# Row rings of seven and eight in place of six and six, a 4 KB descriptor scratch, and routing phases ten slots earlier

## The chip, the cores and the metric

The kernel runs on one core of one Trainium2 chip. The metric is device time in microseconds (us) from start to end of one execution; the lower, the better. Besides the tensor engine (PE), the core has a vector engine (DVE), a scalar engine (ACT), GpSimd (POOL), and a sync engine (SP), which here only issues transfers. All arithmetic is in float32.

## The reference

The program is a decoder trunk of two layers over 512 tokens of width 1024. Each layer has three parallel mixers and then a retrieval mixer with 16384 experts of one neuron each:

```python
for l in range(DEPTH):                      # 2 layers
    h = rms_norm(x, norm1_w[l])
    z, xbc, dt_raw, sb_qkv, nsa_q, nsa_kv, nsa_gate = split(h @ w_in[l])
    mixed = concatenate([ssd, stick_breaking, nsa]) @ w_out[l]
    x = x + mixed
    x = x + peer_ffn(rms_norm(x, norm2_w[l]), peer_w_q[l], peer_sub_keys[l], peer_u[l], peer_v[l])

def peer_ffn(h, ...):                       # per token, 8 heads, 16 experts of each
    q = (xb @ w_q).reshape(Tb, 8, 2, 128)
    sv, si = top_k(q . sub_keys, 16)        # for both halves of a head
    cv, ci = top_k(all 16 x 16 sums, 16)    # the chosen experts: eidx, their gates: softmax(cv)
    u, v = u_tab[eidx], v_tab[eidx]         # two rows of 1024 floats for each token and expert
    a = gelu(sum(u * x));  out = sum(g * a * v)
```

## The kernel before

**Slots.** The tokens go through each layer in two pairs of 128-token blocks, so there are four steps (`STEPS`). A step's retrieval has 256 slots (`PER_STEP`: two blocks of 8 heads by 16 experts). In slot s, GpSimd issues one indirect transfer that gathers row u of one expert for each of 128 tokens (128 rows of 4 KB, one tile `u_rows`), and one that gathers row v of the expert of slot s - 20 (`LAG`, tile `v_rows`). So there are 1024 gathers of u (L1473) and 1024 of v (L1486). DVE multiplies each u tile with the normalised tokens `h2` and sums it (L1412, the dot product). A v tile is taken up either by PE (L750, four matmuls with a diagonal of the weights into `acc`, 682 tiles) or by DVE (L1430, 342 tiles), as `BY_VECTOR` says: every second one in most of a step, one in sixteen while slot + 20 is under 90.

**Rings.** `u_rows` has `U_RING` = 6 tiles and `v_rows` has `V_RING` = 6. GpSimd issues everything in one order, u of slot s and then v of slot s - 20. It waits for the tile's last reader, and at the first slot of a head also for the head's indices:

```python
if s % TOPK == 0 and head <= PEER_H:
    pool.wait_ge(sig("idx"), nth(n, "idx", 2 * head + 1 if head < PEER_H else 2 * PEER_H))
if s >= U_RING:
    pool.wait_ge(sig("u_used"), s - U_RING + 1)
```

**The trunk beside it.** All other work of a step (norms, projections, the three mixers, output projection, query projection and routing) is cut into some 250 named phases. `slots()` gives each phase a slot (`SLOT_OF`), and each engine, after its retrieval work of slot s, does the phases with a slot up to s (`run.upto(phases_after(s))`). Each engine is in order, so the table sets the order of its whole program. A step's phases up to `FIRST` = `r8` are spread over slots 90 to 254 of the step before it (`TRUNK_AT`, `FIRST_AT`), in proportion to their costs; those from `r8` on over its own slots 1 to 86 (`ROUTED_AT`). In the first step nothing runs beside the phases up to `FIRST`.

**Routing.** Phases `r4` to `r22` choose the experts: round k (`r{k}`, `r{k}b`, `r{k}c` on DVE) takes the top 16 of one half of a head, the top 16 of the sums of one block two rounds later, and writes the indices (`chosen`, L1377) one round after that. The indices of head h, block 0, which GpSimd waits for before slot 16 h, come behind `r{7 + 2h}c`.

**Weights.** SP loads 25 blocks of 1 MB a step through a ring of three (L1511), each when PE is done with the block three before it.

**Descriptors.** Transfers of GpSimd have their descriptors written to a scratch in the on-chip memory. Its size is 16384 bytes of each partition unless the program says otherwise.

Of the kernel before, what the change touches and what calls it, by code (L numbers as in the profile page):

```python
# [16 lines left out]
PEER_H, TOPK, KEYS = 8, 16, 128  # L17
# [16 lines left out]
STEPS = DEPTH * PAIRS  # L34
PAIR = 2 * P
PER_STEP = 2 * SLOTS
GATHERS = STEPS * PER_STEP
U_RING, V_RING, DIAG_RING = 6, 6, 5
LAG = TOPK + 4

DIAG_LEAD, POOL_LAG = 2, 4


ROUTED_AT, TRUNK_AT, FIRST_AT = 86, 90, PER_STEP - 2


def of_vector(t):

    step, slot = divmod(t, PER_STEP)
    if slot + LAG < TRUNK_AT:  # L50
        return t % 16 == 15
# [135 lines left out]
PHASES = phases()  # L187
ORDER = {name: i for i, (name, *_) in enumerate(PHASES)}
# [3 lines left out]
FIRST = ORDER["r8"]  # L192


def slots():


    work = np.array([max(cost) + .5 for _, *cost in PHASES[:FIRST]] + [cost[1] + .5 for _, *cost in PHASES[FIRST:]])
    spread = lambda part, lo, hi: lo + (np.cumsum(part) - part) / part.sum() * (hi - lo)
    before_, beside = spread(work[:FIRST], TRUNK_AT - PER_STEP, FIRST_AT - PER_STEP), spread(work[FIRST:], 1, ROUTED_AT)  # L200
    out = [n * PER_STEP + np.concatenate([before_ if n else np.full(FIRST, -1), beside]) for n in range(STEPS)]
    return np.concatenate(out)


SLOT_OF = slots()
assert (np.diff(SLOT_OF) >= 0).all()

assert all(SLOT_OF[ORDER[f"r{7 + 2 * h}c"]] <= 16 * h - 5 for h in range(1, PEER_H))


PER = dict(diag1=2, carry=1, conv=8, xbc=8, dtp=1, dt_log=1, dtA=1, acs=1, ed=1, sb_ln=4, softplus=4, x_dt=2, x_dec=2,
# [5 lines left out]
def trunk(nc, x_dram, const_dram, param_dram, w_dram, u_dram, v_dram, out_dram):  # L217
# [4 lines left out]
    with ctx:  # L222
# [138 lines left out]
        def made(ins, name):  # L361
            given[name] = given.get(name, 0) + 1
            return ins.then_inc(sig(name), 1)
# [62 lines left out]
        def phases_after(slot):  # L426

            return int((SLOT_OF <= slot).sum())
# [307 lines left out]
        def tensor_program(pe):  # L736
            run = Phases(lambda n: tensor_tracks(pe, n))
            run.upto(phases_after(-1))
            for s in range(GATHERS + LAG):
                t = s - LAG  # L740
                at_t = t % SLOTS
# [268 lines left out]
        def scalar_program(act):  # L1010
            chain = InOrder(act, "scalar_chain")
            run = Phases(lambda n: scalar_tracks(act, n, chain))
            run.upto(phases_after(-1))
            for s in range(GATHERS + LAG):
                if s % TOPK == 0 and 0 < s <= GATHERS:
# [4 lines left out]
                    made(S.activation(gel[:, b % 2, at_s:at_s + TOPK], dots[:, b % 2, at_s:at_s + TOPK], ACT.Gelu), "gelu")  # L1020
                t = s - LAG + DIAG_LEAD
                if 0 <= t < GATHERS and not BY_VECTOR[t]:
# [369 lines left out]
        def vector_program(dve):  # L1392
            chain = InOrder(dve, "vector_chain")
            run = Phases(lambda n: vector_tracks(dve, n, chain))
            run.upto(phases_after(-1))
            for s in range(GATHERS + LAG):
                n = s // PER_STEP
# [162 lines left out]
```

## Time and profile before

| | |
|---|---|
| median of 3 runs | 3394.51 us (3392.7 to 3396.86) |
| the profiled execution's own time | 3384.28 us |
| span of the profiled execution | 3382.5 us |
| mean granted TensorE clock | 0.896 of full speed |
| busy: PE, DVE, POOL, ACT | 2623.9, 2455.5, 2313.6, 810.0 us |
| moved by the DMA engines | 1187.52 MB, mean 351 GB/s |

The span runs from the first to the last instruction. The profiled execution took 1.8 us more than its span, and 10.2 us (0.3%) less than the median of the runs. GpSimd is counted busy while it makes a gather's descriptors; about 0.3 us more pass between two of them in any case (releaser "issue").

### The profile page before, as it was taken

To read this page: it belongs to the slowest core of one execution; us is meant where nothing else is said; L and a number is where in the kernel's file an instruction comes from. 1 tells how busy PE (TensorE), PEld (TensorE's weight loads), DVE (VectorE), ACT (ScalarE), POOL (GpSimd) and SP (SyncE) were. 2 spreads that over 40 slices of the span, in tenths; PEclk is the share of its full clock that TensorE was granted. 3 is DMA by queue.
4 is the path that set the end of the run, shared out by engine and by line. 5 is a ranking of instruction groups with operands and counts; after the bars stand their busy time and mean duration, and the time that the engine had idled before them with its cause. 6 is when DMAs were issued, how large, how long until landed. Compare 5 with 4: busy or idle time off the path is not lost.

```text
span 3382.5 us, 30188 instructions
## 1 busy us (share of the span) xinstructions
PE 2623.9 (78%) x8860; PEld 1549.2 (46%) x8860; DVE 2455.5 (73%) x5632; ACT 810.0 (24%) x1860; POOL 2313.6 (68%) x2059
## 2 busy tenths in 40 slices
PE   8896767998896866887887776788988586666667
PEld 7775323665463422654454432565556342222222
DVE  2326996777868986768777997768777998566664
ACT  2521222144321212233321121233431121111111
POOL 0002777767776787767775777767777678777776
PEclk9868899998998898998898899999899899888888
DMA  4115999999999999999999999999999999999999
GB/s 183 62 41 193 360 368 375 412 410 354 347 399 355 365 340 389 411 411 368 348 390 365 387 369 359 388 411 343 356 370 411 351 358 337 363 408 408 409 409 360
DMA packets 311314, 1187.52 MB, mean 351 GB/s; under 512 B 34544, under 2 KB 34544, under 8 KB 298352
## 3 DMA queue, kind: packets, MB, share of 16 engines
q0 software_dynamic: 294912, 1073.87, 83.3%
q1 hardware_dynamic: 16240, 111.72, 8.3%
q8 instruction: 73, 1.20, 0.1%
q14 instruction: 89, 0.73, 0.1%
HBM read 1183.36 MB, written 2.10 MB: 350 GB/s over the span
## 4 chain that ended last, share of the span: by engine, by line
POOL 33%; PE 22%; DMA 20%; issue 11%; DVE 6%; ACT 1%; DVEq 0%; ACTq 0%; POOLq 0%
DMA v_rows<-expert_v,idx 18%; POOL v_rows L1486 17%; POOL u_rows L1473 16%; PE acc L750 13%; PE bank L469 3%; PE bank L460 3%; DMA u_rows<-expert_u,idx 2%; DVE u_rows L1412 2%; PE bank L632 1%; DVE X L1430 1%; PE bank L451 1%; DVE arena L1036 1%; DVE arena L1286 0%; DVE arena L1294 0%; DVE arena L1298 0%
## 5 line engine op out<-in xcount | busy, mean ns | idle before, releaser
L750 PE MATMUL acc<-v_rows,diag 128*128 128x512 f32 x2728 | 1489.1, 683 | 672.6 <-DMA v_rows<-expert_v,idx 598.3
L1412 DVE CUSTOM_DVE_ANT_0 u_rows<-u_rows,h 128x1024 f32<-128x1024 f32 x1024 | 1243.2, 1222 | 540.2 <-DMA u_rows<-expert_u,idx 535.6
L1473 POOL DMA_INDIRECT u_rows<-expert_u,idx x1024 | 1134.1, 1108 | 625.0 <-issue 303.2
L1486 POOL DMA_INDIRECT v_rows<-expert_v,idx x1024 | 1177.0, 1149 | 385.6 <-issue 259.4
L750 PEld LDWEIGHTS acc<-v_rows,diag 128*128 128x128 f32 x2728 | 534.4, 212 | 1417.0 <-issue 1181.4
L1430 DVE SCALAR_TENSOR_TENSOR X<-v_rows,wgt,X 128x1024 f32<-128x1024 f32 x342 | 439.7, 1286 | 73.6 <-DMA v_rows<-expert_v,idx 67.1
L1028 ACT ACTIVATE diag<-consts,wgt 128x128 f32<-128x128 f32 x682 | 256.1, 395 | 850.8 <-PE acc L750 644.2
L460 PE MATMUL bank<-HT,w_ring 128*128 128x256 f32 x1792 | 412.9, 386 | 3.2 <-DVE HT L1036 3.2
L460 PEld LDWEIGHTS bank<-HT,w_ring 128*128 128x128 f32 x1792 | 350.0, 196 | 97.7 <-issue 53.4
L469 PE MATMUL bank<-w_ring,HT 128*128 128x256 f32 (+1 forms) x1280 | 274.6, 371 | 0.0
L469 PEld LDWEIGHTS bank<-w_ring,HT 128*128 128x128 f32 x1280 | 237.1, 191 | 52.5 <-issue 24.4
L761 ACT ACTIVATE arena<-bank 128x256 f32<-128x256 f32 (+4 forms) x304 | 113.2, 383 | 600.3 <-PE bank L460 210.1
L1020 ACT ACTIVATE gel<-dots 128x16 f32<-128x16 f32 x64 | 13.8, 216 | 417.8 <-DVE dots L1412 417.6
L1036 DVE TENSOR_TENSOR arena<-arena 128x256 f32<-128x256 f32 (+3 forms) x238 | 102.1, 432 | 4.6 <-ACT arena L761 3.5
L1412 DVE DVE_READ_ACCUMULATOR2_ANT dots<- 128x1 f32 x1024 | 83.8, 82 | 0.0
L1020 ACT ACT_TABLE_LOAD x51 | 65.4, 1283 | 0.9
L1286 DVE MAX8 arena<-arena 128x8 f32<-128x128 f32 (+1 forms) x192 | 52.8, 327 | 15.6 <-ACT arena L761 13.4
L682 PE MATMUL bank<-nkT,arena 64*128 64x128 f32 (+3 forms) x128 | 59.3, 549 | 5.2 <-ACT arena L957 5.2
L957 ACT ACTIVATE arena<-bank,sm_nm 128x128 f32<-128x128 f32 (+3 forms) x64 | 33.7, 526 | 120.8 <-DVE sm_nm L1235 57.7
L451 PE MATMUL bank<-dg,X 128*128 128x128 f32 x256 | 40.3, 329 | 25.9 <-ACT dg L761 25.9
L1294 DVE MATCH_REPLACE8 arena<-arena 128x128 f32<-128x128 f32 (+1 forms) x192 | 59.5, 319 | 0.0
L1036 DVE TENSOR_TENSOR arena<-arena,consts 128x256 f32<-128x256 f32 (+3 forms) x168 | 58.4, 386 | 0.7
(186 smaller groups left out, 1971.6 us busy)
## 6 DMA issues: line engine op xcount, KB each, us to landing
w_ring<-weights SPq DMA_DIRECT2D x100, 1024.0 KB, 8.0
u_rows<-expert_u,idx POOLq DMA_INDIRECT x1024, 6.7
v_rows<-expert_v,idx POOLq DMA_INDIRECT x1024, 6.8
X<-in_x SPq DMA_DIRECT2D x2, 1024.0 KB, 6.5
out<-X SPq DMA_DIRECT2D x4, 512.0 KB, 6.1
n2w_wide<-parameters SPq DMA_DIRECT2D x2, 512.0 KB, 8.0
params<-parameters SPq DMA_DIRECT2D x2, 412.0 KB, 8.0
consts<-constants SPq DMA_DIRECT2D x1, 749.5 KB, 6.4
```

What stands on the lines that cost most here:

```text
L451: last = T.matmul(out[:, blk[i]], src[:, k * P:(k + 1) * P], dg[:, at_d + b], start=True, stop=True)
L460: last = T.matmul(out[:, 0:PAIR], cols(i)[:, k, m % 2 * P:(m % 2 + 1) * P], HT[:, k, :], start=(k == 0), stop=(k == KT - 1))
L469: last = T.matmul(out[:, 0:width], HT[:, k, blk[b]], cols(i)[:, k, 0:width], start=(k == 0), stop=(k == KT - 1))
L750: last = T.matmul(acc[:, at_h], diag[:, i % DIAG_RING], v_rows[:, t % V_RING, at_h], start=(at_t == 0), stop=(t == max(q for q in range(t ...
L761: return S.activation(dst, src, ACT.Copy, **k)
L1020: made(S.activation(gel[:, b % 2, at_s:at_s + TOPK], dots[:, b % 2, at_s:at_s + TOPK], ACT.Gelu), "gelu")
L1028: made(S.activation(diag[:, i % DIAG_RING], ident, ACT.Copy, scale=wgt[:, b % 2, at_t:at_t + 1]), "diag")
L1036: return V.tensor_tensor(out, in0, in1, op)
L1412: made(V.tensor_tensor_reduce(out=rows_u, in0=rows_u, in1=h2[:], scale=1.0, scalar=0.0, op0=ALU.mult, op1=ALU.add, accum_out=dots[:, b % 2 ...
L1430: made(V.scalar_tensor_tensor(Xb, v_rows[:, t % V_RING, :], wgt[:, b % 2, at_t:at_t + 1], Xb, ALU.mult, ALU.add), "v_used_vector")
L1473: pool.indirect_dma_start(out=u_rows[:, s % U_RING, :], out_offset=None, in_=u_dram, in_offset=bass.IndirectOffsetOnAxis(ap=idx[:, n % 2, ...
L1486: pool.indirect_dma_start(out=v_rows[:, t % V_RING, :], out_offset=None, in_=v_dram, in_offset=bass.IndirectOffsetOnAxis(ap=idx[:, t // PE ...
```

## The change

Three things change. The ring of u tiles gets a seventh and the ring of v tiles a seventh and eighth: three tiles of 4 KB per partition, 12 KB. The scratch for descriptors goes from 16384 to 4096 bytes per partition, which frees the same 12 KB. And `FIRST_AT` goes from 254 to 246: the phases up to `r7c` are spread over slots 90 to 246 of the step before, and the phases from `r8` on begin at slot 246 of that step (-10) and end at 86 as before. The first step's own phases from `r8` stay at 1 to 86.

```diff
--- before.py
+++ after.py
@@ -35,13 +35,15 @@
 PAIR = 2 * P
 PER_STEP = 2 * SLOTS
 GATHERS = STEPS * PER_STEP
-U_RING, V_RING, DIAG_RING = 6, 6, 5
+U_RING, V_RING, DIAG_RING = 7, 8, 5
 LAG = TOPK + 4
 
+SCRATCH = 4096
+
 DIAG_LEAD, POOL_LAG = 2, 4
 
 
-ROUTED_AT, TRUNK_AT, FIRST_AT = 86, 90, PER_STEP - 2
+ROUTED_AT, TRUNK_AT, FIRST_AT = 86, 90, PER_STEP - 10
 
 
 def of_vector(t):
@@ -197,15 +199,17 @@
 
     work = np.array([max(cost) + .5 for _, *cost in PHASES[:FIRST]] + [cost[1] + .5 for _, *cost in PHASES[FIRST:]])
     spread = lambda part, lo, hi: lo + (np.cumsum(part) - part) / part.sum() * (hi - lo)
-    before_, beside = spread(work[:FIRST], TRUNK_AT - PER_STEP, FIRST_AT - PER_STEP), spread(work[FIRST:], 1, ROUTED_AT)
-    out = [n * PER_STEP + np.concatenate([before_ if n else np.full(FIRST, -1), beside]) for n in range(STEPS)]
+    alone = np.full(FIRST, -1), spread(work[FIRST:], 1, ROUTED_AT)
+    beside = spread(work[:FIRST], TRUNK_AT - PER_STEP, FIRST_AT - PER_STEP), spread(work[FIRST:], FIRST_AT - PER_STEP, ROUTED_AT)
+    out = [n * PER_STEP + np.concatenate(beside if n else alone) for n in range(STEPS)]
     return np.concatenate(out)
 
 
 SLOT_OF = slots()
 assert (np.diff(SLOT_OF) >= 0).all()
 
-assert all(SLOT_OF[ORDER[f"r{7 + 2 * h}c"]] <= 16 * h - 5 for h in range(1, PEER_H))
+assert all(SLOT_OF[n * len(PHASES) + ORDER[f"r{7 + 2 * h}c"]] <= n * PER_STEP + 16 * h - (10 if n else 5)
+           for n in range(STEPS) for h in range(1, PEER_H))
 
 
 PER = dict(diag1=2, carry=1, conv=8, xbc=8, dtp=1, dt_log=1, dtA=1, acs=1, ed=1, sb_ln=4, softplus=4, x_dt=2, x_dec=2,
@@ -1551,7 +1555,7 @@
     a = {name: np.ascontiguousarray(v) for name, v in inputs.items()}
     arrays = {"in_x": a["x"], "constants": constants(), "parameters": parameters(a), "weights": weight_slots(a),
               "expert_u": a["peer_u"].reshape(DEPTH * EXPERTS, D), "expert_v": a["peer_v"].reshape(DEPTH * EXPERTS, D)}
-    nc = bacc.Bacc("TRN2", target_bir_lowering=False, num_devices=1)
+    nc = bacc.Bacc("TRN2", target_bir_lowering=False, num_devices=1, dynamic_dma_scratch_size=SCRATCH)
     drams = [nc.dram_tensor(name, t.shape, mybir.dt.float32, kind="ExternalInput").ap() for name, t in arrays.items()]
     out = nc.dram_tensor("out", (1, SEQ, D), mybir.dt.float32, kind="ExternalOutput").ap()
     trunk(nc, *drams, out)
```

Slots of some phases of a step, counted from the step's own slot 0, worked out from `slots()`:

```
phase        n1a     u0     t8    mt0     r0     r6    r7c     r8    r9c    r13c   r22c
before    -166.0 -162.2  -63.2  -41.6  -23.4   -9.5   -3.1    1.0   10.1   32.6   83.2
after     -166.0 -162.4  -68.2  -47.7  -30.3  -17.1  -11.1  -10.0    0.3   25.7   82.8
```

GpSimd's program has the same instructions, and its gathers stand in the same order. On DVE the order changes. This is the place where the second step's first indices are made, in slot 253 of the first step before (`ISA u_rows,dots` is the dot product of one slot, L1412, and `idx<-arena` the indices):

```order
L1412 ISA u_rows,dots<-u_rows,h2 128x1024
L1412 ISA dots 128x1
L1430 SCALAR_TENSOR_TENSOR X<-v_rows,wgt,X 128x1024
L1303 MAX_INDEX si<-arena 128x8 x2
L1303 MAX_INDEX ci<-arena 128x8
L1324 TENSOR_REDUCE arena<-arena 128x16 x2
L1351 CAST arena<-si 128x32
L1355 TENSOR_SCALAR ch<-ci 128x16
L1356 TENSOR_SCALAR ch<-ci 128x16
L1357 CAST arena<-ch 128x2x16
L1036 TENSOR_TENSOR g<-arena 128x2x16
L1377 TENSOR_SCALAR idx<-arena 128x16
```

After the change the same instructions stand behind the dot product of slot 245, eight slots earlier (lines are four higher in the changed file), and what stands behind the dots of slots 253 to 255, which had no phases behind 253, is work of round `r9`:

```order
L1416 ISA u_rows,dots<-u_rows,h2 128x1024
L1416 ISA dots 128x1
L1434 SCALAR_TENSOR_TENSOR X<-v_rows,wgt,X 128x1024
L1298 MATCH_REPLACE arena<-arena 128x128 x2
L1298 MATCH_REPLACE arena<-arena 128x256
L1040 TENSOR_TENSOR arena<-arena 128x256
L1302 MAX arena<-arena 128x8 x3
L1040 TENSOR_TENSOR arena<-arena 128x256
L1409 SCALAR_TENSOR_TENSOR h2<-X,sm_rs5,n2w_wide 128x1024
```

There it stood before as two readers of rows and the tokens of the next block alone:

```order
L1412 ISA u_rows,dots<-u_rows,h2 128x1024
L1412 ISA dots 128x1
L1412 ISA u_rows,dots<-u_rows,h2 128x1024
L1412 ISA dots 128x1
L1430 SCALAR_TENSOR_TENSOR X<-v_rows,wgt,X 128x1024
L1405 SCALAR_TENSOR_TENSOR h2<-X,sm_rs5,n2w_wide 128x1024
```

So DVE has routing work in the last ten slots of a step that it had in the next step's first slots, and the work of those ten slots has moved ahead of them.

## Rows read from the trace of the kernel before

**Rows 1.** The page's slices (40 of 84.6 us): DMA share in tenths, GB/s

```profile
DMA  4115999999999999999999999999999999999999
GB/s 183 62 41 193 360 368 375 412 410 354 347 399 355 365 340 389 411 411 368 348 390 365 387 369 359 388 411 343 356 370 411 351 358 337 363 408 408 409 409 360
```

**Rows 2.** Windows: busy us (instructions) of each engine, granted clock, DMA share, GB/s

```profile
core 0: us, PE busy (x) PEld busy (x) DVE busy (x) ACT busy (x) POOL busy (x), PEclk, DMA share, GB/s
600.00:700.00 100.00, 90.59 (x351) 64.92 (x350) 69.39 (x108) 24.67 (x54) 72.13 (x64) 0.97 1.02 411
700.00:770.00 70.00, 66.36 (x273) 43.02 (x274) 58.09 (x94) 34.11 (x70) 50.08 (x47) 0.98 1.02 404
820.00:960.00 140.00, 121.75 (x529) 74.71 (x528) 106.78 (x185) 48.97 (x110) 110.87 (x93) 0.88 0.97 355
...
1010.00:1070.00 60.00, 39.14 (x135) 25.12 (x134) 50.35 (x146) 8.60 (x24) 34.22 (x30) 0.83 0.90 354
1070.00:1130.00 60.00, 43.05 (x115) 24.25 (x114) 56.89 (x168) 7.81 (x22) 46.48 (x43) 0.80 0.99 376
1130.00:1210.00 80.00, 67.68 (x199) 35.70 (x197) 78.23 (x268) 18.35 (x44) 63.73 (x53) 0.98 0.96 352
3110.00:3290.00 180.00, 123.00 (x209) 45.75 (x208) 110.19 (x163) 20.75 (x56) 137.33 (x141) 0.84 1.03 409
```

**Rows 3.** Waits of POOL over the whole span: total us, times, longest

```profile
POOL u_rows L1473 <- DVE idx L1377: 299.1, 8, 248.4
POOL v_rows L1486 <- PE acc L750: 123.3, 170, 4.3
POOL u_rows L1473 <- DVE dots L1412: 22.4, 19, 2.1
```

**Rows 4.** Timeline of POOL at the first step's end: start, us, instruction, idle before

```profile
1047.16 0.95 POOL L1486 DMA_INDIRECT v_rows<-expert_v,idx  x1 [0.30 <-issue]
1061.75 1.67 POOL L1473 DMA_INDIRECT u_rows<-expert_u,idx  x1 [13.65 <-DVE idx L1377]
```

**Rows 5.** Waits of DVE in 1040:1110, 1826:1896 and 2616:2686

```profile
DVE u_rows L1412 <- DMA u_rows<-expert_u,idx: 4.2, 2, 2.8
DVE u_rows L1412 <- DVE h L1405: 0.6, 1, 0.6
...
DVE u_rows L1412 <- DMA u_rows<-expert_u,idx: 3.8, 2, 3.1
DVE u_rows L1412 <- DVE h L1405: 0.5, 1, 0.5
...
DVE u_rows L1412 <- DMA u_rows<-expert_u,idx: 2.3, 1, 2.3
DVE X L1430 <- DMA v_rows<-expert_v,idx: 2.1, 2, 1.2
DVE u_rows L1412 <- DVE h L1405: 0.7, 1, 0.7
```

**Rows 6.** Gathers of u in 600:700, then in 3110:3290, from issue to landing

```profile
DMA to landing us min/median/max: 11.5/15.4/18.8
...
DMA to landing us min/median/max: 7.8/7.9/8.2
```

**Rows 7.** Waits of POOL for PE in 720:860, 1510:1650 and 2295:2440

```profile
POOL v_rows L1486 <- PE acc L750: 5.7, 3, 4.0
...
POOL v_rows L1486 <- PE acc L750: 3.7, 4, 1.8
...
POOL v_rows L1486 <- PE acc L750: 6.0, 3, 3.5
```

**Rows 8.** Group of L750 on the page: busy us, mean ns, idle before

```profile
L750 PE MATMUL acc<-v_rows,diag 128*128 128x512 f32 x2728 | 1489.1, 683 | 672.6 <-DMA v_rows<-expert_v,idx 598.3
```

**Rows 9.** The queue of GpSimd's transfers, and all gathers of v by duration

```profile
q0 software_dynamic: 294912, 1073.87, 83.3%
...
L1486 POOL DMA_INDIRECT v_rows<-expert_v,idx x1024: 932/988/4215, 341.3 to 3370.7; - x171
```

## The prediction

> **What bounds the kernel now.** I read the page's slices first, then windows of 60 to 180 us, then GpSimd's waits, then the timeline at one step's end.
>
> The slices show the DMA share at 9 from the fifth on, but the rate moves between 337 and 412 GB/s [rows 1]: the engines always have something outstanding, and only in some slices is the rate at its top. The windows say who sets the pace [rows 2]:
> - In 600:700 and 700:770 the share is 1.02 and the rate 411 and 404 GB/s, while GpSimd is busy 72 of 100 us. The transfers are saturated there (weights come beside the gathers). A u gather lands 15.4 us after its issue [rows 6].
> - In 820:960 the rate is 355 GB/s, and GpSimd is busy 110.87 us with 93 gathers. With 0.3 us between gathers that is 138.8 of 140 us: GpSimd's issuing sets the pace, 1.51 us a gather. In 1130:1210 it is 79.6 of 80 us, and DVE is busy 78.2 of those 80 too.
> - In 3110:3290, the last step without a trunk beside it, both limits are met at once: 409 GB/s, and 137.3 + 42.3 = 179.6 of 180 us on GpSimd, 1.28 us a gather. A gather lands in 7.9 us [rows 6], so about six are under way and no ring is full. Nothing that the change touches is at work in this stretch.
> - At a step's end, 1010:1070, GpSimd issues 30 gathers where it issues 40 in other 60 us, and the rate falls to 354 GB/s.
>
> GpSimd waits 299.1 us for indices [rows 3], of which 248.4 are the program's start. The other 50.7 us are nearly all at the three ends of steps. The timeline has one: 13.65 us before the gather at 1061.75 [rows 4]. It also waits 123.3 us for PE and 22.4 us for DVE to free a tile [rows 3]; where the transfers are saturated, such waits cost nothing.
>
> **Part 1, the indices eight slots earlier.** They stood behind DVE's slot 253. With six tiles, GpSimd may issue the first u of a step when DVE has done slot 250, so it was late by three slots, the 13.65 us. After the change they stand behind slot 245, and with seven tiles GpSimd needs them after slot 249: four slots to spare, and the wait is gone. But GpSimd's wait isn't DVE's. During it the queue of landed and outstanding rows fed DVE, which was busy with routing: DVE is busy 50.4 and 56.9 us of the two windows of 60 us [rows 2]. Behind the gap DVE waited only 4.2 + 0.6, 3.8 + 0.5 and 2.3 + 2.1 + 0.7 us at the three ends [rows 5]. That sum, **14 us**, is what the bubble cost the path. The rest of the 50.7 us had cover: DVE's own work.
>
> **Part 2, the deeper rings.** While the transfers are saturated, or DVE or PE holds the pace, three more tiles only make the gathers wait longer for landing. They pay on leaving such a stretch: GpSimd is then up to three gathers further, and from there its issuing is the pace. Three gathers at 1.51 us are 4.5 us. There are six such exits: behind the start of each of steps 2 to 4, and behind the saturated stretch in the middle of steps 1 to 3. That makes **27 us**. A check for the middle ones: GpSimd's waits for PE around these exits are 5.7, 3.7 and 6.0 us [rows 7], 15.4 together, and I take 13.5 of them. From below the whole part is nothing, if PE or DVE uses the lead up at once.
>
> **Part 3, routing moved out of GpSimd's stretch.** A gather occupies GpSimd 1.20 us on average in 1130:1210 (63.73 / 53), beside DVE's routing, but 0.97 us in 3110:3290 (137.33 / 141) [rows 2]. The extra 0.23 us on some 170 gathers of slots 1 to 86 is 39 us a step, 2.6 us for each of 15 rounds. 1.6 rounds now stand ahead of slot 0, where GpSimd has time to spare: 4 us a step, 12 in all. The first thirty slots are DVE's pace anyway, so I take half, **6 us**.
>
> **Part 4, the trunk in 156 slots instead of 164.** Each phase up to `r7c` now has 5% fewer slots. PE is the engine that this meets: in 700:770 it is busy 66.4 of 70 us. The v tiles cost it 1489.1 / 682 = 2.18 us each [rows 8], 1.09 a slot; 47 gathers are 23.5 slots, so PE has 2.82 us a slot, 1.73 of them trunk. 5% of that is 0.09 us; over the 64 slots or so at this load, 5.6 us a step. PE's idle time hides much of it, and deeper rings help. I take 2 us for three steps, **6 us lost**. On DVE the rounds `r4` to `r7` get denser too, but they move to where DVE waits for saturated transfers (it is busy 69 of 100 us in such a stretch [rows 2]), so I cost that at nothing; without that cover it would be some 3 us a step.
>
> **Part 5, the smaller scratch.** The page counts 294912 packets for 2048 gathers [rows 9], 144 a gather, 9 for each of 16 engines. No row shows a wait for room in the scratch. From below it costs nothing. From above: one gather took 4215 ns where the median is 988 [rows 9]; if a scratch that is too small added those 3.2 us each time the ring of eight comes round, 128 times, it would be 410 us. I take nothing, because at most 15 gathers can be alive at once now, and 12 before, with a median issue 56 ns above the shortest; the 410 us are the rival below.
>
> The Trainium skill (DMA: Bandwidth & Descriptors, Terms and The descriptor swizzle) has descriptors of 16 bytes and 9 read and 9 write descriptors per engine for such a transfer; the trace's 9 packets agree. By that page, as an estimate, 4096 bytes hold 256 descriptors, so 28 gathers, more than the 15.
>
> The first step's routing keeps its slots, and a seventh u tile lets GpSimd reach slot 16 a slot earlier, only to wait for the same index: nothing. Weight loads move with PE's phases, SP being ahead of them.
>
> **Sum.** -14 - 27 - 6 + 6 = -41 us. The profiled execution took 3384.3 us, so 3343; the median of the runs stands 10.2 us above it, so **3353 us**.
>
> **Rivals.**
> - *Only the bubble goes* (0.2). DVE is so full at a step's start (78.2 of 80 us) that the lead is used up there, and PE (90.6 of 100 us) does the same in the middle. For it: those two shares. Against it: GpSimd at 138.8 of 140 us in the middle. Then -14 to -16: 3380.
> - *GpSimd gains all that it waits* (0.1). 50.7 us for indices and, outside saturated stretches, 15.4 for PE and about 10 for DVE come back whole: 3394.5 - 76 = 3318. Against it: DVE's stall of 14 us for 50.7 us of wait.
> - *PE becomes the bound* (0.06), the slower side. If the 5% fell on PE with no idle left over all 156 slots, with 1.53 us of trunk a slot (820:960: 121.75 / 46.5 - 1.09), it would be 0.05 x 1.53 x 164 = 12.5 us a step, 38 in all. The exits then give nothing, and 14 us come back: 3394.5 + 24 = 3418. It decides once PE is at 98% or more through the trunk; it is at 87 to 95% now [rows 2].
> - *The scratch is too small* (0.03): GpSimd waits for room, up to the 410 us above, 3760.
> - *The transfers have nothing left* (0.02). Mean traffic is 351 GB/s; if about that were the ceiling, no earlier issue could help, and the time would stay at 3394. Rows at 409 to 412 GB/s over whole slices speak against it [rows 1]. The same page of the Trainium skill (Where 436 GB/s comes from) says that the HBM side binds at about 358 GB/s for such loads; by that rule the 1187.5 MB need 3317 us, and next to nothing would be won. The trace doesn't agree: one core alone moves 411.
>
> **How the numbers follow.** The likeliest case has 0.59; its own range, by taking part 2 between a half and the whole and part 4 between nothing and its 17 us, is 3338 to 3378. Range with the neighbours: 3322 to 3386, which leaves out the slower cases and the lowest. A change of under 0.2% (6.8 us) can't be told from none. Faster by more: most of the first three cases, 0.85. Within it: 0.08. Slower: 0.07.
>
> **What would show it.** In the changed profile GpSimd's wait for indices is about 250 us instead of 299, and its wait for PE is shorter; DVE's waits behind the three ends are gone; a u gather in the first saturated stretch takes 18 to 19 us to land instead of 15.4; in 3110:3290's counterpart nothing differs; the mean gather on GpSimd is equal or a little shorter. I am wrong if the GpSimd-paced stretch runs at another pace than 1.51 us a gather, if PE has no idle time in the trunk, or if issues get longer at regular distances.

## The result

| | median | lowest to highest | runs |
|---|---|---|---|
| before | 3393.61 us | 3386.8 to 3396.86 | 4 |
| changed | 3339.62 us | 3332.65 to 3348.83 | 4 |

The ratio is 0.9845, 95% interval [0.9814, 0.9876]: faster by 54 us, where 41 were forecast; 3339.6 lies in the range. The changed kernel was timed once more beside the last experiments: ratio 0.9857 [0.9824, 0.9889], median 3335.13 against 3385.24 us, so 50 us.

The profiled execution took 3332.65 us, span 3330.9 (before: 3384.28 and 3382.5). The slices of its page answer to [rows 1]:

```profile
DMA  4115999999999999999999999999999999999999
GB/s 185 64 38 189 343 363 376 412 410 372 361 399 395 341 352 364 410 412 383 376 382 410 367 385 364 387 412 389 367 364 411 379 345 367 379 409 410 409 409 373
```

The top rate is what it was, 409 to 412 GB/s. What changed is how often it is reached: the mean is 357 GB/s instead of 351 over a span that is 51.6 us shorter.

GpSimd's waits over the whole span of the changed kernel, which answer to [rows 3]:

```profile
POOL u_rows L1477 <- DVE idx L1381: 255.4, 3, 248.4
POOL u_rows L1477 <- DVE dots L1416: 90.2, 65, 2.6
POOL v_rows L1490 <- PE acc L754: 58.6, 139, 4.2
```

Of the 50.7 us of waits for indices behind the start, 7 are left. Those for PE have halved, those for DVE are four times as long: GpSimd now stands longer at the u ring, behind DVE, and for less time at the v ring, behind PE. The gather that came after the gap of 13.65 us [rows 4], the first u of the second step, now follows the one ahead of it at the usual distance, and no wait around it is longer than 2.2 us:

```profile
1048.21 0.94 POOL L1477 DMA_INDIRECT u_rows<-expert_u,idx  x1 [0.31 <-issue]
```

In the windows of DVE's waits behind the three ends, which held 4.8, 4.3 and 5.1 us [rows 5], DVE has no wait at all now. Windows of the changed kernel: the last two rows are slots 240 to 256 of the first step, and 0 to 32 of the second.

```profile
600.00:700.00 100.00, 89.68 (x348) 64.48 (x347) 67.70 (x106) 27.88 (x61) 73.37 (x67) 0.97 1.02 412
820.00:960.00 140.00, 128.50 (x535) 81.39 (x534) 110.68 (x193) 42.34 (x98) 109.66 (x96) 0.92 0.99 374
1012.00:1068.00 56.00, 36.23 (x105) 19.83 (x105) 53.74 (x161) 7.63 (x18) 39.79 (x34) 0.86 1.02 402
1068.00:1159.50 91.50, 64.87 (x179) 35.80 (x178) 90.18 (x273) 16.60 (x40) 69.01 (x61) 0.82 0.95 343
3060.00:3240.00 180.00, 115.77 (x210) 40.61 (x211) 109.67 (x162) 20.42 (x56) 137.30 (x141) 0.91 1.03 409
```

The last step's stretch is the same to a tenth (137.30 us and 141 gathers in 180 us, as in [rows 2]). At the step's end DVE is busy 53.7 of 56 and 90.2 of 91.5 us, which makes it the likely path there; experiment 3 tests that.

**Where the 51.6 us came from.** The starts of DVE's dot products (L1412, L1416 after) mark the slots, so that the two traces can be cut at equal work. Length of each stretch in us, by ends of steps 1, 2, 3 (for the trunk: steps 1, 2, 3):

```
stretch                          before                 after            saved
end: slot 240 to next 32    155.0  156.1  155.2   147.2  147.3  146.8     25.0
start: slot 32 to 96        191.3  184.5  189.7   191.4  178.1  181.0     14.9
slot 96 to 144              157.0  153.0  156.4   156.4  153.0  158.4     -1.4
trunk: slot 144 to 240      287.8  286.7  294.3   286.6  284.7  286.4     11.1
first 96 slots, last step from 96, tail behind the last dot                1.9
```

The rows of the ends repeat within 1 us; in a second profile of the changed kernel they were 147.2, 146.9 and 147.1. The other rows move by several us from one execution to the next (second profile: 193.2, 186.5, 181.0 and 281.5, 284.0, 286.9), so 14.9 and 11.1 have an error of 8 us or more each: against the second profile they would be 4.8 and 16.5. Of the last row, the tail behind the last dot gives 3.6 us and the first 96 slots lose 1.8.

What the ends gained is not work taken off DVE. These are the sums over the three stretches from slot 240 to slot 32, in the kernel before and in the changed one:

```profile
sum 466.30, PE 336.80 PEld 196.45 DVE 428.10 ACT 70.20 POOL 322.28; mean PE 112.27 PEld 65.48 DVE 142.70 ACT 23.40 POOL 107.43
```

```profile
sum 441.30, PE 300.10 PEld 165.83 DVE 430.53 ACT 72.66 POOL 326.30; mean PE 100.03 PEld 55.28 DVE 143.51 ACT 24.22 POOL 108.77
```

DVE is busy 428 us before and 431 us after, but it stands idle 38 us before and 11 us after. The whole gain is idle time of DVE. Some of that idle time lay ahead of the gap: from slot 240 (1012.2) to 1040, DVE waited 5.5 us for rows of u to land, and 6.7 and 5.3 us in the other two ends.

### The profile page after: what moved, and what is told of

The parts are those of the page before. It is cut to its first block, busy times and chain, and to the rows that moved or that the text cites. A ratio compares the mean times of both kernels' runs of the same rounds, so it can differ in the third digit from the quotient of the medians.

```text
span 3330.9 us, 30181 instructions
## 1 busy us (share of the span) xinstructions
PE 2586.4 (78%) x8860; PEld 1528.7 (46%) x8860; DVE 2448.9 (74%) x5632; ACT 800.1 (24%) x1853; POOL 2305.6 (69%) x2059
## 4 chain that ended last, share of the span: by engine, by line
POOL 31%; DMA 22%; PE 16%; DVE 13%; issue 11%; ACT 1%; DVEq 0%; ACTq 0%; POOLq 0%
POOL u_rows L1477 16%; DMA v_rows<-expert_v,idx 16%; POOL v_rows L1490 15%; PE acc L754 10%; DMA u_rows<-expert_u,idx 6%; DVE u_rows L1416 4%; DVE X L1434 2%; PE bank L464 1%; DVE arena L1040 1%; PE bank L473 1%; PE bank L636 1%; DVE arena L1298 1%; DVE arena L1302 1%; DVE arena L1290 1%; PE bank L455 1%
## 5 line engine op out<-in xcount | busy, mean ns | idle before, releaser
L754 PE MATMUL acc<-v_rows,diag 128*128 128x512 f32 x2728 | 1461.0, 670 | 644.8 <-DMA v_rows<-expert_v,idx 538.4
L1416 DVE CUSTOM_DVE_ANT_0 u_rows<-u_rows,h 128x1024 f32<-128x1024 f32 x1024 | 1242.8, 1223 | 501.7 <-DMA u_rows<-expert_u,idx 499.5
L1477 POOL DMA_INDIRECT u_rows<-expert_u,idx x1024 | 1153.1, 1126 | 636.8 <-issue 290.9
L1490 POOL DMA_INDIRECT v_rows<-expert_v,idx x1024 | 1150.0, 1123 | 328.5 <-issue 269.6
L754 PEld LDWEIGHTS acc<-v_rows,diag 128*128 128x128 f32 x2728 | 525.5, 209 | 1386.8 <-issue 1115.5
L1416 DVE DVE_READ_ACCUMULATOR2_ANT dots<- 128x1 f32 x1024 | 84.3, 82 | 0.0
L455 PEld LDWEIGHTS bank<-dg,X 128*128 128x128 f32 x256 | 40.1, 243 | 43.9 <-issue 43.9
```

The costliest lines, as they stand in the source:

```text
L455: last = T.matmul(out[:, blk[i]], src[:, k * P:(k + 1) * P], dg[:, at_d + b], start=True, stop=True)
L754: last = T.matmul(acc[:, at_h], diag[:, i % DIAG_RING], v_rows[:, t % V_RING, at_h], start=(at_t == 0), stop=(t == max(q for q in range(t ...
L1416: made(V.tensor_tensor_reduce(out=rows_u, in0=rows_u, in1=h2[:], scale=1.0, scalar=0.0, op0=ALU.mult, op1=ALU.add, accum_out=dots[:, b % 2 ...
L1477: pool.indirect_dma_start(out=u_rows[:, s % U_RING, :], out_offset=None, in_=u_dram, in_offset=bass.IndirectOffsetOnAxis(ap=idx[:, n % 2, ...
L1490: pool.indirect_dma_start(out=v_rows[:, t % V_RING, :], out_offset=None, in_=v_dram, in_offset=bass.IndirectOffsetOnAxis(ap=idx[:, t // PE ...
```

## The experiments

Each of the twelve runs is set against the kernel before on the same chip (medians between 3385 and 3387 us).

**1. Four parts, each alone.** The rings and the scratch with the old slots:

```diff
-U_RING, V_RING, DIAG_RING = 6, 6, 5
+U_RING, V_RING, DIAG_RING = 7, 8, 5
+    ..., dynamic_dma_scratch_size=4096)
```

> Rings of seven and eight with the 4 KB scratch, all phases in the slots that they have in the kernel before. My theory (the parts of the prediction add up): the six exits give up to 27 us and the tail of the program, which was 3.6 us shorter in the changed kernel, gives 3 to 4; the wait for indices at the three ends stays near 13 us each, shortened by nothing, since the indices stand behind slot 253 all the same. So 20 to 31 us below the kernel before, ratio 0.991 to 0.994. Rival (the rings only help together with the earlier indices, since the idle queue at a step's end drains whatever lead there is): only the three exits in the middle and the tail remain, 5 to 12 us, ratio 0.9965 to 0.9985.

Measured: 0.9937 [0.9908, 0.9966], median 3367.38 us. The whole is as my theory had it. By stretches, the ends are 155.2, 156.0 and 155.8 us, not a microsecond better, with 309.8 us of waits for indices left. The rest came behind the ends (32 to 96: 193.3, 180.8, 181.1), in the trunk (288.2, 280.1, 285.1) and in the tail. GpSimd's waits for PE fell from 123.3 to 48.7 us, but 42 us of that fall lie in slots 96 to 144, where the transfers are saturated and nothing was saved; in the trunk they fell from 15 to 5 us:

```profile
POOL u_rows L1477 <- DVE idx L1381: 309.8, 8, 248.1
...
POOL u_rows L1477 <- DVE dots L1416: 54.1, 38, 2.9
POOL v_rows L1490 <- PE acc L754: 48.7, 137, 1.8
```

The slots alone, with six and six tiles and the 16 KB scratch:

```diff
-ROUTED_AT, TRUNK_AT, FIRST_AT = 86, 90, PER_STEP - 2
+ROUTED_AT, TRUNK_AT, FIRST_AT = 86, 90, PER_STEP - 10
-... spread(work[FIRST:], 1, ROUTED_AT)
+... spread(work[FIRST:], FIRST_AT - PER_STEP, ROUTED_AT)
```

> The new table of slots (FIRST_AT 246, rounds from r8 at slot 246) with rings of six and six and the 16 KB scratch. My theory: the bubble's 14 us and the moved routing's 6 us come, 6 us are lost by the denser trunk: 10 to 20 us below the kernel before, ratio 0.994 to 0.997. Rival: the step's start is the whole gain and needs no deeper ring (40 of the 52 us between the two profiles lie between slot 240 and slot 96 of the next step): 30 to 40 us below, ratio 0.988 to 0.991.

Measured: 0.9969 [0.9946, 0.9993], median 3377.29 us. The number is within my theory's, but not for its reason. The ends are at 147.9, 146.9 and 147.0 us: the gain of the changed kernel there, 24.5 us, and it needs no deeper ring, as the rival had it. But the trunk went from 287.8, 286.7, 294.3 to 301.6, 298.1, 294.0 us, and GpSimd's waits for PE in it from 15 to 33 us. (This profiled execution was 13 us above its kernel's median, so a part of that is its own.)

The scratch alone:

```diff
-    nc = bacc.Bacc("TRN2", ..., num_devices=1)
+    nc = bacc.Bacc("TRN2", ..., num_devices=1, dynamic_dma_scratch_size=4096)
```

> Only the scratch goes from 16384 to 4096 bytes; rings, slots and everything else as before. My theory: no row showed a wait for room, so nothing: within 0.2% of before, mean gather on GpSimd 1.11 and 1.15 us as before. Rival: room runs short or reclaiming it more often costs something at each turn of the scratch; then longer gathers at regular distances, and a ratio above 1.002.

Measured: 0.9992 [0.9972, 1.0011]. Nothing, as expected. Its profile serves as a second one of the kernel before: the ends are 154.8, 155.9 and 154.2 us, slots 32 to 96 188.5, 186.9 and 183.9, the trunk 286.9, 291.7 and 296.0.

The first part of the new table alone. The indices are as early as in the changed kernel, but no round stands in the last ten slots:

```diff
-ROUTED_AT, TRUNK_AT, FIRST_AT = 86, 90, PER_STEP - 2
+ROUTED_AT, TRUNK_AT, FIRST_AT = 86, 90, PER_STEP - 10
 ... spread(work[FIRST:], 1, ROUTED_AT)
```

> The phases up to r7c end at slot 246, so that the first indices stand behind slot 245, but the phases from r8 on begin at slot 1 as before; rings of six and six, 16 KB scratch. My theory: the bubble's 14 us come, less 2 us a step for the denser trunk: 5 to 14 us below the kernel before, ratio 0.996 to 0.9985; the difference to the run with the whole table is what the moved rounds are worth, 6 us. Rival: moving the rounds from r8 on is what pays (DVE's queue at the step's start is the path): then this one is within 0.2% of before, and the whole table is far better than it.

Measured: 0.9892 [0.9858, 0.9926], median 3346.07 us. Both expectations fail: this is 37 us, more than either allowed and better than the whole table with the same rings. The ends take 144.2, 143.3 and 145.3 us, 11 less than before each. The first 16 slots of such an end, from the start of slot 240's dot product to that of the next step's first, in the kernel before and in this one:

```profile
1012.00:1067.00 55.00, 36.13 (x124) 22.83 (x122) 48.21 (x145) 7.67 (x21) 30.25 (x27) 0.84 0.89 355
```

```profile
1020.00:1066.00 46.00, 24.36 (x55) 10.87 (x53) 41.46 (x101) 5.58 (x15) 35.01 (x31) 0.85 1.00 392
```

DVE has 41.5 us of work there instead of 48.2, and the stretch is 9 us shorter. The work moved ahead costs nothing visible: slots 224 to 240 take 51.0 us (before: 51.3), where the transfers are saturated (DMA share 1.02, 411 GB/s). Over the whole ends, the slots alone and this run compare so:

```profile
sum 441.70, PE 306.18 PEld 168.92 DVE 430.00 ACT 72.66 POOL 332.36; mean PE 102.06 PEld 56.31 DVE 143.33 ACT 24.22 POOL 110.79
```

```profile
sum 432.80, PE 300.27 PEld 160.26 DVE 407.51 ACT 64.16 POOL 334.54; mean PE 100.09 PEld 53.42 DVE 135.84 ACT 21.39 POOL 111.51
```

Against the kernel before (428 us of work, 38 us idle), this run has 21 us less of DVE's work and 13 us less of its idle time in the three ends. Starting round `r8` ten slots ahead of slot 0, as slots_alone does, brings 22 us of other rounds into these slots; 14 of them fill idle time, and the other 9 us make the ends longer.

**2. One ring at a time, and the best parts together.** The changed kernel with seven u and six v tiles:

```diff
-U_RING, V_RING, DIAG_RING = 7, 8, 5
+U_RING, V_RING, DIAG_RING = 7, 6, 5
```

> The changed kernel with seven u tiles but six v tiles. Without either extra ring the new table gave 0.9969 of before, with both 0.9845. Theory A (a lead of so many gathers at the exit of a stretch, whichever ring holds them): one of three extra tiles, so about a third of the 42 us, ratio near 0.993. Theory B (PE, slow in the middle of the trunk, holds GpSimd's one queue at a v tile, and with it DVE's u rows): the u tile alone does next to nothing, ratio 0.995 to 0.998.

Measured: 0.9964 [0.9931, 0.9997]. That is the slots alone (0.9969): the u tile by itself gives nothing that can be told from none, as theory B said. With six u and eight v tiles:

```diff
-U_RING, V_RING, DIAG_RING = 7, 8, 5
+U_RING, V_RING, DIAG_RING = 6, 8, 5
```

> The changed kernel with six u tiles and eight v tiles. Theory A (lead): two of three extra tiles, but GpSimd's queue alternates, so u at six caps the lead at once: ratio near 0.994. Theory B (PE's delays are taken up by the v ring): most of the 42 us between 0.9969 and 0.9845 come back, ratio 0.985 to 0.988.

Measured: 0.9924 [0.9894, 0.9954]: some 15 us better than the slots alone, not the 42 of both rings. So neither theory holds by itself. GpSimd's waits show where it stands. Seven and six:

```profile
POOL v_rows L1490 <- PE acc L754: 133.6, 158, 7.1
...
POOL u_rows L1477 <- DVE dots L1416: 12.3, 10, 2.2
```

Six and eight:

```profile
POOL u_rows L1477 <- DVE dots L1416: 132.7, 96, 4.1
```

GpSimd issues u and v in turns from one queue, so a full ring holds up the gathers of the other one too: with six v tiles it waits 133.6 us for PE, with six u tiles 132.7 us for DVE. With both rings deeper the two waits are 58.6 and 90.2 us. In the trunk alone GpSimd waits 32 us for PE with seven and six, 29 us for DVE with six and eight, and 20 us for both together in the changed kernel.

The early indices without rounds in the last ten slots, with both rings:

```diff
 U_RING, V_RING, DIAG_RING = 7, 8, 5
-... spread(work[FIRST:], FIRST_AT - PER_STEP, ROUTED_AT)
+... spread(work[FIRST:], 1, ROUTED_AT)
```

> Rings of seven and eight with the 4 KB scratch, phases up to r7c ending at slot 246, phases from r8 on from slot 1: the run first_early (0.9892) with the deeper rings. If the parts add up (rings alone gave 0.9937), the ratio is 0.983, at or a little below the changed kernel: the step's end is shorter by 3 to 4 us than in the changed kernel and the rings' gain in the trunk is the same. Rival: the early index and the deeper rings remove the same waits, so the ratio stays at 0.987 to 0.989 and the rounds from r8 on in the last ten slots are what the deeper rings pay for in the changed kernel.

Measured: 0.9793 [0.9758, 0.9827], median 3313.84 us. The parts add up (0.9892 by 0.9937 is 0.9830, just above the interval's end and well within the errors of the two factors), and this kernel is faster than either: by medians 72 us below the one before, and 21 to 26 below the changed one, though the intervals of the last two still touch. The ends, which repeat best, give 18 us of that: they take 141.1, 141.1 and 140.9 us, the trunk 284.8, 284.1 and 287.4. DVE's work in the ends is that of first_early (407 us), its idle time 16 us instead of 25.

The changed kernel with half of its scratch:

```diff
-SCRATCH = 4096
+SCRATCH = 2048
```

> The changed kernel with a scratch of 2048 bytes. By the count of 9 packets per engine in a gather and descriptors of 16 bytes (the Trainium skill, DMA: Bandwidth & Descriptors) it holds 14 gathers, fewer than the 15 that the rings of seven and eight let live. Theory: room in the scratch is what a gather takes from issue to landing, not to its use; 10 to 13 are under way in saturated stretches and 4 to 6 elsewhere, so the time is that of the changed kernel within 0.3%. Rival: GpSimd waits for room at each turn of the scratch until all gathers under way have landed: 146 turns by 5 to 15 us, over 700 us more.

Measured: 0.9863 [0.9822, 0.9904], ends 147.2, 147.0, 147.6 us: the changed kernel's time.

**3. Is DVE the path at a step's end?** In the changed kernel, PE takes more of the v tiles there, DVE one in four instead of every second one, as in the last step of both kernels:

```diff
-    return t % 4 == 3 if step == STEPS - 1 else t % 2 == 1
+    return t % 4 == 3 if step == STEPS - 1 or slot + LAG >= FIRST_AT else t % 2 == 1
```

> The changed kernel, but of the v tiles that are taken up from slot 246 of a step to slot 19 of the next, DVE takes one in four instead of every second one; PE takes the others. In the changed kernel DVE is busy 3.34 of 3.48 us a slot over slots 240 to 255, PE 2.2. Theory (DVE is the path there, because the moved rounds meet its v tiles): 30 slots by 0.25 of 1.29 us is 9 us less on DVE at each of three ends, of which some is lost again since a gather takes 2.9 us a slot on GpSimd in any case: slots 240 to 32 take 141 to 144 us instead of 147, and the ratio falls to 0.980 to 0.984. Rival (GpSimd's order and pace hold these slots too): they stay at 146 to 148 us and the ratio at 0.984 to 0.987.

Measured: 0.9816 [0.9782, 0.985], median 3320.4 us; the ends take 138.3, 138.4 and 138.4 us, where 147 stood. So it is: DVE takes 11 v tiles in an end instead of 18, its work there falls by 8.7 us, and the end is 8.7 us shorter. DVE's idle time is what it was, 11 us in the three ends:

```profile
sum 415.20, PE 323.67 PEld 176.70 DVE 404.43 ACT 79.86 POOL 317.43; mean PE 107.89 PEld 58.90 DVE 134.81 ACT 26.62 POOL 105.81
```

PE has 24 us more work in these ends than in the changed kernel's, and they are shorter all the same, so PE isn't the path there. The medians show less of it than the three ends' 26 us: 15 us below the changed kernel timed beside it (3335.13), with intervals that overlap.

The phases up to `r7c` ending at slot 240, in the best kernel of experiment 2:

```diff
-ROUTED_AT, TRUNK_AT, FIRST_AT = 86, 90, PER_STEP - 10
+ROUTED_AT, TRUNK_AT, FIRST_AT = 86, 90, PER_STEP - 16
```

> The run first_early_rings with the phases up to r7c ending at slot 240 instead of 246. If only the wait for the index counted, it would be no better: the index is in time already, and the trunk gets denser by another 4%, 2 to 6 us a step: ratio 0.981 to 0.985. If the gain came from DVE's work taken out of its full slots, another six slots without rounds give another 2 to 4 us at each end, against the denser trunk: ratio 0.977 to 0.980.

Measured: 0.9909 [0.9879, 0.9939]. Both expectations fail. The ends gain more than I thought (133.3, 133.7, 132.8 us, 8 less each), but the trunk takes 308.9, 293.0 and 303.6 us, 24, 9 and 16 more than in the run first_early_rings. The wait for indices isn't the reason (266.9 us in all, 250.4 at the start). GpSimd set the pace of the trunk there, and now it stands at the u ring, behind DVE. Its waits in the first trunk, in first_early_rings and in this run:

```profile
POOL u_rows L1477 <- DVE dots L1416: 0.7, 1, 0.7
```

```profile
POOL u_rows L1477 <- DVE dots L1416: 23.1, 9, 4.7
```

In the other two trunks these waits are 11.1 and 22.1 us (1.1 and 3.2 in first_early_rings), which is most of what each lost, while GpSimd's waits for PE stay under 2 us. PE is busy 87, 82 and 87% of these trunks, less than in first_early_rings (91, 83 and 91%). So the loss comes through DVE, as far as the traces show: it has 10 to 12 us more work in each trunk and is busy 47 of 57 us in slots 224 to 240 of the second. How much of the rest is DVE waiting for other phases was not tested.

The changed kernel with a quarter of its scratch, a single execution:

```diff
-SCRATCH = 4096
+SCRATCH = 1024
```

> The changed kernel with a scratch of 1024 bytes, by the count above room for 7 gathers (64 descriptors of 16 bytes on each engine, 9 a gather). 4 to 6 gathers are under way in most stretches and 10 to 13 in saturated ones, so here GpSimd must wait for room. If room is freed as gathers land, only the saturated stretches show longer issues and the time stays within 1%; if GpSimd waits for all that are under way at each turn, every seventh gather takes 5 us or more and the time rises by 20% to 40%.

Measured: span 3354.6 us, 24 and 19 more than the changed kernel's two profiles. Here room does bite, and mostly where the transfers are saturated: in 600:700 the pauses between gathers that the profile puts down to nothing else (releaser "issue"), 0.3 us at most in the changed kernel, reach 2.2 us, and a u gather lands after 10.4 us (median) instead of 16.7. From these times and 61 and 67 gathers in 100 us, some 6 are under way instead of 11, as an estimate. In 820:960 such pauses stay under 1 us and add up to 28 us, against 29 in the changed kernel.

```profile
POOL u_rows L1477 <- issue: 14.6, 31, 1.9
POOL v_rows L1490 <- issue: 14.6, 28, 2.2
```

The ends aren't slower (147.6, 147.4 and 147.6 us). That fits a wait for single gathers to land, and not one for all that are under way. With one execution, the size of the loss isn't settled.

And the changed kernel once more:

> The changed kernel itself, in the same call as the candidates, since its single profile and its four runs (3332.65 to 3348.83) spread by 0.5%: ratio 0.982 to 0.987, slots 240 to 32 at 147 us three times, the trunk stretch from slot 144 to 240 between 283 and 292 us with its granted clock.

Measured: 0.9857 [0.9824, 0.9889], as told above.

## Why the prediction was right, and by which steps

The direction and the range hold; 41 us were forecast, 54 and 50 measured. The likeliest case's own range is a poorer guide than it looks: its lower end, 3338, doesn't follow from the terms that are named for it. Part 4 at nothing gives 3353 - 6 = 3347, and 3339.6 lies below that. The total is near because errors of opposite sign met in it. By its parts:

- **Part 1, the indices, 14 us: too small.** The wait went as forecast, and DVE's stalls behind it. But the three ends gave 25 us, and the run without deeper rings gave the same. The mis-sized term is this one. It counted DVE's waits behind slot 247 alone. From slot 240 to 32 DVE stood idle 38 us in the three ends, and 27 of them went. The waits ahead of the gap went too, because rounds that had stood behind slot 0 now fill them. Experiment 1 parts the two (in first_early, 13 us of idle time and 21 us of work leave the ends), and experiment 3 shows that what is left is DVE's work, microsecond for microsecond.
- **Part 3, rounds moved out of GpSimd's stretch, 6 us gained: the sign was wrong.** With rounds in the last ten slots the ends take 147 us; without them 144 (six and six tiles) and 141 (seven and eight), so they cost 9 to 18 us. In slots 32 to 96, where the gain should have been, DVE has 8 us less work a step, and no gain beyond the scatter. The rounds were put on DVE where it was the path, to spare GpSimd where it was.
- **Part 2, the deeper rings, 27 us.** With the old slots the size is right (rings alone: 0.9937, 21 us), and it came where forecast: 10 us in slots 32 to 96, 15 us in the trunks behind the saturated stretch, each with an error of 8 us or more. Whether that is a lead of three gathers or PE's delays in the trunk taken up (11 us less waiting there) isn't shown. With the new slots the same rings are worth 42 us (0.9969 to 0.9845). So the term depends on part 4, and most of what the forecast lacks is here. That both rings must grow together I had not seen: eight v tiles with six u tiles give 15 of the 42 us.
- **Part 4, the denser trunk, 6 us lost.** With seven and eight tiles this is right or even too much: the trunk takes 284 to 286 us a step with either table (rings alone 284.5 on average, changed kernel 285.9 and 284.1). With six and six tiles it was 297.9 and 290.1 on average in the two runs with denser trunks (before 289.6, scratch alone 291.5), with 33 and 30 us of waits for PE in it instead of 15, and 10 in the changed kernel. So the deeper rings take up the waits that the density brings; the prediction said only that they help. It also had no step for where the density stops being cheap: in 150 slots it costs 16 us a step.
- **Part 5, the scratch, nothing.** Right: 0.9992 [0.9972, 1.0011] for 4096 bytes, and no loss at 2048.
- **The tail.** I had no term for the 3.6 us behind the last dot product. They belong to the v ring: from the last dot product to the end, every run with eight v tiles takes 33.0 us, every one with six 35.9 to 36.6.
- **The signs to look for.** The wait for indices (255.4 for 250 forecast), the waits behind the ends, the stretch of the last step (7.8/7.9/8.2 us to landing, the same) came as said. In 600:700 a u gather landed after 16.7 us, not 18 to 19. One sign of being wrong did show: in 820:960 GpSimd issued 96 gathers instead of 93 (100 in the second profile), 1.46 us each and not 1.51.

Of the rivals, PE as the bound is not what was seen: even in 150 slots PE is at 82 to 87%, and the loss there comes with waits for DVE. That the transfers had nothing left is refuted: the best median here is 3313.84 us with the same gathers and weights.

What stays open: the runs slots_alone and first_early have the same instructions up to slot 246 of the first step, yet their first trunks took 301.6 and 291.7 us, and their medians differ by 31 us, of which the ends explain 9. The intervals allow a difference as small as some 7 us, so scatter may be all of the rest; the runs can't say. Nor was the table of first_early_rings tried with more v tiles on PE, though the two gains (experiments 2 and 3) concern the same full DVE and need not add.

## What to carry to other kernels

When an engine waits long for an input, look at who is the path around that wait, and count that engine's idle time over the whole stretch and not behind the gap alone: here a wait of 13.65 us on GpSimd showed as 5 us on DVE behind it, while DVE stood idle 12 us in that end. Where two rings are fed in turns from one queue, try them deeper together: one alone gave nothing or 15 us, both 42. A table that makes one stretch denser to lighten another should be tried at several values: with the deep rings the price was nothing that could be measured at 156 slots and 16 us a step at 150.

## What the runs showed of the hardware

- The scratch for descriptors could be cut from 16384 to 2048 bytes without a measurable cost (0.9992 at 4096; 0.9863 at 2048 against 0.9857 for the same kernel at 4096), and at 1024 bytes, in one execution, GpSimd's pauses between gathers grew to 2.2 us in a saturated stretch. The Trainium skill (DMA: Bandwidth & Descriptors, Terms and The descriptor swizzle) gives descriptors of 16 bytes, and 9 of them on either side per engine for a 1 MiB transfer to 128 partitions. A gather here is half that size, and the trace shows 9 packets per engine for it. By these two figures, as an estimate, 2048 and 1024 bytes hold 14 and 7 gathers. The trace fits: 1024 bytes bite where 11 gathers were under way, and hardly elsewhere.
- Stretches where DVE was busy nearly all the time repeated closely: the changed kernel's ends took 146.8 to 147.3 us in both profiles. Its other stretches did not: between the two profiles the same trunk differed by up to 5 us (286.6 and 281.5) and the same slots 32 to 96 by 8 (178.1 and 186.5). What makes them scatter isn't shown.
